# GpSimd's weight splits and its work on the sample states, each operation cut into two or four pieces

## The reference, cut to what matters

```
S_new = exp(g)[..., None] * S + k[..., :, None] * v[..., None, :]   # A, samples: state S (8, 4, 128, 128)
branch = einsum('btnc,ncd->btnd', ys, w_branch)
merged = sum(sigmoid(mg).reshape(B, T, 3, D) * branch, axis=2)
x_new  = layer_norm(ALPHA * x + gate[:, None] * (merged @ w_out), ln_g, ln_b)
```

## Time and profile before

| what | value |
|---|---|
| median of 3 runs | 1674.11 us |
| the profiled execution's own time | 1672.7 us |
| its span, first to last instruction | 1670.9 us |
| mean granted TensorE clock | 0.973 |
| TensorE busy | 1532.8 us, 92% |
| VectorE busy | 883.7 us, 53% |
| ScalarE busy | 563.9 us, 34% |
| GpSimd busy | 472.3 us, 28% |

### The profile page before, as it was taken

One profiled execution on the slowest core, in us unless ns is written; L12 is line 12 of the kernel. 1 busy time (PEld: TensorE's weight loads), 2 busy tenths in 40 slices (PEclk: granted clock), 3 DMA queues, 4 the chain that ended last, 5 costly groups with the idle time before them and its releaser, 6 DMA issues.

```text
span 1670.9 us, 35260 instructions
## 1 busy us (share of the span) xinstructions
PE 1532.8 (92%) x14484; PEld 1373.8 (82%) x14484; DVE 883.7 (53%) x1555; ACT 563.9 (34%) x1128; POOL 472.3 (28%) x461
## 2 busy tenths in 40 slices
PE   5899989989898999999989998999899998999997
PEld 4799866666667888888879998898798887999997
DVE  4660557666651333333334247677763475467588
ACT  1313135555451333333312334546442675001100
POOL 1122001000003111112031367677672131234500
PEclk9899989999999999999989999999999999999999
DMA  9411120000006243343233311212032020544322
GB/s 333 154 39 53 27 89 2 1 1 1 2 27 180 78 131 115 115 119 115 69 122 103 116 38 40 66 40 79 27 119 68 26 79 30 200 152 166 139 90 77
DMA packets 136850, 143.19 MB, mean 86 GB/s; under 512 B 17110, under 2 KB 126706, under 8 KB 135922
## 3 DMA queue, kind: packets, MB, share of 16 engines
q1 hardware_dynamic: 127362, 127.03, 24.8%
q10 hardware_dynamic: 9328, 13.90, 2.3%
HBM read 115.62 MB, written 29.40 MB: 87 GB/s over the span
## 4 chain that ended last, share of the span: by engine, by line
PE 52%; DVE 8%; ACT 6%; issue 2%; POOL 1%; DMA 0%; SPq 0%; DVEq 0%; ACTq 0%; PEldq 0%; POOLq 0%
PE ps L1012 42%; PE ps L1361 2%; DVE xq L2566 1%; ACT xq L2031 1%; PE ps L1374 1%; PE ps L1023 1%; PE ps L1561 1%; ACT srw L1948 1%; DVE att L2583 1%; ACT L1928 1%; PE ps L1568 1%; PE ps L1657 1%; DVE sel L2450 1%; PE ps L1402 0%; PE ps L1575 0%
## 5 line engine op out<-in xcount | busy, mean ns | idle before, releaser
L1012 PE MATMUL ps<-w_hi,h_hi 128*128 128x256 f32 x704 | 205.0, 291 | 6.8 <-DVEq L152 2.6
L1012 PE MATMUL ps<-h_hi,w_hi 128*128 128x344 f32 x600 | 199.8, 333 | 4.7 <-POOL w_lo L902 1.7
L1012 PE MATMUL ps<-w_lo,h_hi 128*128 128x256 f32 x704 | 200.2, 284 | 1.4 <-issue 1.4
L1012 PE MATMUL ps<-w_hi,h_lo 128*128 128x256 f32 x704 | 200.1, 284 | 0.0
L1012 PE MATMUL ps<-h_lo,w_hi 128*128 128x344 f32 x600 | 193.9, 323 | 0.0
L1012 PE MATMUL ps<-h_hi,w_lo 128*128 128x344 f32 x600 | 193.4, 322 | 0.0
L1012 PE MATMUL ps<-h_hi,wg_hi 128*128 128x344 f32 x432 | 145.0, 336 | 16.4 <-ACT gate_stage L1902 15.5
L1012 PEld LDWEIGHTS ps<-w_hi,h_hi 128*128 128x128 f32 x704 | 135.4, 192 | 11.0 <-DVEq L152 3.1
L901 POOL CAST w_hi<-w_raw 128x1024 fp32r<-128x1024 f32 (+1 forms) x48 | 52.9, 1102 | 318.6 <-DMA w_raw<-in_w_in 127.2
L1012 PE MATMUL ps<-h_lo,wg_hi 128*128 128x344 f32 x432 | 139.0, 322 | 0.0
L1012 PE MATMUL ps<-h_hi,wg_lo 128*128 128x344 f32 x432 | 138.8, 321 | 0.0
(11 more groups left out here) (463 smaller groups left out, 3569.3 us busy)
## 6 DMA issues: line engine op xcount, KB each, us to landing
w_raw<-in_w_in SPq DMA_DIRECT2D x46, 512.0 KB, 4.7
sgm<-gate_spill SPq DMA_DIRECT2D x22, 516.0 KB, 6.3
gate_spill<-gate_stage ACTq DMA_DIRECT2D x54, 172.0 KB, 2.4
w_raw<-in_w_in SPq DMA_DIRECT2D x34, 256.0 KB, 4.2
adw<-in_ada_w SPq DMA_DIRECT2D x8, 1024.0 KB, 11.4
pgc<-in_cache_nsa_kv SPq DMA_DIRECT2D x64, 128.0 KB, 2.8
pg<-in_cache_nsa_kv SPq DMA_DIRECT2D x64, 128.0 KB
w_raw<-in_w_branch SPq DMA_DIRECT2D x12, 512.0 KB, 5.9
```

What stands on the lines that cost most here:

```text
L1012: last = mm(out, lhsT=l, rhs=r, start=(first and i == 0 and j == 0), stop=(final and i == n - 1 and j == 2), skip_group_check=joint)
```

## The change

Each cast of a half is made in two instructions and each remainder in four, in `split_half` and in the loop over the gate units. Each cast piece is waited for; the remainder pieces are issued without a wait between them, and only the last counts up `half_split`. In `sample_states` each of the three large operations is made in four pieces of two samples each, with a wait after each piece; the last signals `sts_done`. Nothing else changes.

```
@@ split_half
-            st(nc.gpsimd.tensor_copy(hi[:, k, 0:width], raw))
-            st.fire(nc.gpsimd.tensor_tensor(lo[:, k, 0:width], raw, hi[:, k, 0:width].bitcast(F32), SUB), half_split)
+            for j in (0, 2):
+                kj = slice(4 * hf + j, 4 * hf + j + 2)
+                last = nc.gpsimd.tensor_copy(hi[:, kj, 0:width], raw[:, j:j + 2])
+                st(last)
+            for j in range(4):
+                kj = slice(4 * hf + j, 4 * hf + j + 1)
+                last = nc.gpsimd.tensor_tensor(lo[:, kj, 0:width], raw[:, j:j + 1], hi[:, kj, 0:width].bitcast(F32), SUB)
+                st.fire(last, half_split if j == 3 else own["pool"])
@@ gate units
-            st(nc.gpsimd.tensor_copy(hi, raw))
-            st.fire(nc.gpsimd.tensor_tensor(lo, raw, hi.bitcast(F32), SUB), half_split)
+            for j in (0, 4):
+                st(nc.gpsimd.tensor_copy(hi[:, j:j + 4], raw[:, j:j + 4]))
+            for j in range(0, 8, 2):
+                st.fire(nc.gpsimd.tensor_tensor(lo[:, j:j + 2], raw[:, j:j + 2], hi[:, j:j + 2].bitcast(F32), SUB), half_split if j == 6 else own["pool"])
@@ sample_states
-            st(nc.gpsimd.tensor_tensor(STS, STS, decay.unsqueeze(2).to_broadcast([P, NS, P]), MUL))
+            for b in range(0, NS, 2):
+                st(nc.gpsimd.tensor_tensor(STS[:, b:b + 2], STS[:, b:b + 2], decay[:, b:b + 2].unsqueeze(2).to_broadcast([P, 2, P]), MUL))
             pool.wait_ge(vb_in, vs_before + 16 * (h + 1))
-            st(nc.gpsimd.tensor_tensor(VB, VB, k.unsqueeze(2).to_broadcast([P, NS, P]), MUL))
-            st(nc.gpsimd.tensor_tensor(STS, STS, VB, ADD), e("sts_done"))
+            for b in range(0, NS, 2):
+                st(nc.gpsimd.tensor_tensor(VB[:, b:b + 2], VB[:, b:b + 2], k[:, b:b + 2].unsqueeze(2).to_broadcast([P, 2, P]), MUL))
+            for b in range(0, NS, 2):
+                st(nc.gpsimd.tensor_tensor(STS[:, b:b + 2], STS[:, b:b + 2], VB[:, b:b + 2], ADD), e("sts_done") if b == NS - 2 else None)
```

## The result

The changed kernel took 1666.17 us, median of 6 runs (1662.60 to 1667.59), beside 1673.60 us for the kernel before (6 runs, 1672.11 to 1676.77); the ratio is 0.9949, 95% interval 0.9936 to 0.9963. It is faster, by 7.4 us by the medians and 8.5 by the ratio, whose interval allows 6 to 11. The forecast was no change, at 1674.6.

What follows compares the result with a forecast made beforehand. TensorE, busy 92% of the span, was taken to bound the kernel. Terms -3.0 - 2.8 - 0.1 + 2.8 + 0.8 + 2.5 + 0.3 = +0.5 us on 1674.11 gave 1674.6 (chance 0.40), range 1666 to 1682.

Steps and rivals of the forecast that it cites:

- the first part: What bounds the kernel: the change can give back only TensorE idle time that ends with a late VectorE.
- The signs that the working named: Remainder pieces near 0.74 us, no `xq` above 1.1, branch A stalls about 4, new sum waits, longer w_lo waits.
- the merge's term: Merge: 0.1 us gained, 2.2 from h_lo less 2.1 for a later sgm load; bounds 2 gained, 3 lost.
- Branch A: Branch A's heads: 3.0 us gained as VectorE's products end earlier, less later sums of the states; bounds 0 and 9.
- What is late next: Branch A: the sum of the states comes 6.2 us later, so the sample output starts 1.9 us earlier, not 3.5.
- the fourth unit of B: Fourth unit of B, where TensorE waits for GpSimd's remainder: 2.5 us lost, bounds 1.5 and 4.5.
- the first gate unit: First gate unit, which TensorE waits for: 0.8 us lost.
- the samples' attention: Samples' attention, tiny `sel` operations behind whole remainders: 2.8 us gained, bounds 0 and 5.
- Unit cg: Unit cg, whose last remainder TensorE awaits without cover: 2.8 us lost, reaching the end; bounds 1.4 and 4.
- The faster one: Rival: sample states ready in time, splits in B and cg held less than reckoned; 8 us faster, 1666; chance 0.27.
- The rival of the turns: GpSimd loses a full VectorE instruction per turn at B, cg, merge and states' sum: near 1683 at worst; chance 0.23.
- The block: Rival: four unwaited remainder pieces hold the port as one, so trains still wait about 2.8 us; 1678; chance 0.10.

Runs made afterwards that it cites:

- e1: Kernel before, with pieces in the casts and remainders of the first unit alone, all else whole: ratio 0.9984 to the kernel before.
- e5: Changed kernel, with whole casts and remainders in the first unit and pieces everywhere else: ratio 0.9983 to the kernel before.
- e10: Changed kernel, with whole casts and remainders in the merge's units: ratio 0.9956 to the kernel before.
- e4: Changed kernel, with whole casts and remainders in unit cg, the first gate unit and the fourth unit of B: ratio 0.9915 to the kernel before.
- e7: Kernel before, with remainders in four pieces in every split, casts and states whole: ratio 0.9953 to the kernel before.
- e8: e4, with the states' pieces issued without waits between them: 1655.92 us, ratio 0.9903 to the kernel before.
- e2: Kernel before, with pieces in the three operations on the samples' states alone, all splits whole: ratio 0.9980 to the kernel before.
- e9: e8, with all GpSimd casts whole, so only remainders and states in pieces: ratio 0.9926 to the kernel before.
- e11: e9, with only the first of the states' three operations in pieces, the other two whole: ratio 0.9953 to the kernel before.
- e3: Changed kernel, with the states' operations whole and all splits in pieces: ratio 0.9942 to the kernel before.
- e12: e9, with remainders and the states' operations in two pieces instead of four: ratio 0.9956 to the kernel before.

## Why the prediction was wrong

**The step that failed** is in the first part: TensorE idles that "end with a late VectorE" were looked for in branch A, the samples and the merge, and never in the first 50 us. The earlier trace rows leave out the row that was larger than two of the three used: 9.2 us of TensorE's waits for `mod_rows`. The start was priced at nothing without naming what covers it; it gave some 3 to 5 us (e1, e5, and the first-projection column), in the profiled execution 2.6 of VectorE's turns and 1.6 of clock. The signs that the working named came nearly all: pieces of 0.61 and 0.74 us, no product above 0.79, the stalls at 5.1, the new waits for the sum and for w_lo, only smaller at cg (1.7 for 3). They lay where it had looked, and so could not show what it had left out.

**The second** is the merge's term, 0.1 gained. The working took 2.2 us off the `h_lo` wait and gave 2.1 back for a later `sgm`. VectorE did wait longer for `sgm` (5.53 us before its product, 2.22 in the earlier trace rows), but regained it: the pause went from 2.54 to 1.68 us, and with it went the low clock behind it, which the sum didn't contain. Together 2 to 2.7 us (e10).

**Branch A**: sign and mechanism right, the terms rough. The working had 0.9, 1.9, 0.4, 0.7 and -0.9 for heads 0 to 4; the trace gives 2.2 and 4.3 gained, then 1.2, 0.7 and 0.3 lost. What is late next was named and came, in three heads: the sum ended 7.7 us after x_ready in head 1 (1029.77 against the product at 1022.06), where the working had 8.6 and the room was 7.1. It cost 0.4 us there and 2.6 in head 3. Head 1's gain of 4.3 was put at 1.9: the stall shrank by 3.85 us (5.68 to 1.83) where the working had 3.5, the new wait is 0.4 where it had 1.6, and the remaining 0.9 go with the granted clock behind the stall (0.59 and 0.66 in two stretches of 5 us before, 0.77 in one after), which was not in it. In head 4, where it expected a wait of 0.9 for the sum, none came. Head 2 lost 1.2 us with a granted clock of 0.74 in the stretch at 1100; e4 shows it too, but e5 and e10, with the same program in branch A, show none there, so it does not follow from the pieces alone.

**Right in size**: the fourth unit of B (+3.0 for 2.5, and 3.2 in e4), the first gate unit (0.7 for 0.8), the samples' attention (2.1 for 2.8; three samples gained 0.57 to 0.59 each where the working took 0.5), four remainders in 2.92 us (2.97) and two casts in 1.37 (1.42). Unit cg cost 1.8, then 0.9 of it came back; the working had 2.8 and said that nothing would come back.

**The rivals.** The faster one gives 1666, the time that came, but not by its reasons, so that it met the time is chance: the states were not ready in time, and B lost what the forecast had, not less. The rival of the turns fails at its place: pieces of GpSimd lost much to VectorE, but the 1 to 4 us of each place came out near the forecast. The block is refuted (e7). The sum of -3.0 - 2.8 - 0.1 + 2.8 + 0.8 + 2.5 + 0.3 needs -4 for the start and about -2.5 for the end of the merge, and then gives -6, where 7.4 by the medians and 8.5 by the ratio were measured. By the stage table cg lost 1.9 less and branch A gained 1.3 more than the sum has, while B lost 1.5 more and the samples gained 0.7 less, which makes -7; what is left is within the noise of the measurement.

## What to carry to other kernels

When two engines take turns on whole instructions, cut the long instruction of the engine with slack to the length of the short ones beside it, and only where the other engine is late: here the same edit loses 5.8 us where TensorE waits for the cut work itself. Before pricing such a change, list every stretch in which both engines are busy, the program's start and end included, and ask in each who waits for either. A pause removed can take with it a fall of the clock that the trace shows behind it, and that can be worth as much again, as in the merge here.

## What the runs showed of the hardware beyond that

GpSimd yields to VectorE between two pieces whether it waits behind the first or not (e7's remainders without waits let the split of h in after 1.41 us; in e8, without waits, two pieces of `vs_spread` took 2.59 us beside the scan and nine of the sixteen 0.61 or 0.62). Of TensorE's pauses before the last merge units, those of 1.85 to 2.56 us (before, e1, e2, e9, e10, e11) have a stretch of granted clock 0.66 to 0.70 behind them, those of 0.46 to 1.72 us (the changed kernel, e3 to e8, and the shortest, e12) have none. That is a list of fourteen pauses at one place and not a rule.
